# Paged sample attention: small loads issued in the sparse stage, keys turned in halves, branch rows combined in halves by VectorE and GpSimd

## What is computed

```python
sc = jnp.where((jnp.arange(n_keys)[None, :] <= qpos[:, None])[None], indexer_scores(qi, wi, ki_all), -jnp.inf)
_, sel = lax.top_k(sc, topk)                      # 256 of the 1028 keys of a request
kv_past = pool_kv[phys, sel_p % PAGE_SIZE]        # rows of the paged cache, phys from the page table
kv_sel = jnp.where(in_past[..., None, None, None], kv_past, kv_cur)
return sparse_attend(qa, kv_sel[:, :, :, 0], kv_sel[:, :, :, 1], valid)
```

```python
wts = jax.nn.softmax(jnp.stack(lses, axis=0), axis=0)
o = jnp.einsum('gbth,gbthd->bthd', wts, jnp.stack(outs, axis=0).astype(jnp.float32))
```

## Time and profile before

| | |
|---|---|
| median of 3 runs | 2304.71 us (2299.87 to 2311.17) |
| the profiled execution | 2307.14 us, of which the span is 2305.4 us |
| TensorE busy | 2114.3 us, 92% of the span |
| VectorE, ScalarE, GpSimd busy | 1175.4, 621.3, 518.2 us |
| mean granted TensorE clock | 0.943 of full speed |
| `attend_sample_a` | from about 1092.7 to 1185.1 us |

### The profile page before, as it was taken

How to read it: one execution, slowest core, us unless ns; L and a number is a source line. 1 busy time by engine, 2 the same in 40 slices (tenths; PEclk the granted TensorE clock), 3 DMA queues, 4 the chain that set the end, 5 groups by cost and what they waited for, 6 DMA issues and landing times. The chain is left out here.

```text
span 2305.4 us, 32999 instructions
## 1 busy us (share of the span) xinstructions
PE 2114.3 (92%) x12535; PEld 1945.7 (84%) x12535; DVE 1175.4 (51%) x2287; ACT 621.3 (27%) x1247; POOL 518.2 (22%) x569
## 2 busy tenths in 40 slices
PE   5999899999998976898669989989999999999997
PEld 5878788999998864555359988889999999999997
DVE  5049999998720413542337232644344444444445
ACT  5243222121210752343122233631121111111112
POOL 4786656778820001100000120210000000000000
PEclk9999999999986966999789998999999999999999
DMA  4122222357632444871337202030112110111001
GB/s 154 28 85 75 66 85 82 110 165 250 210 122 88 124 136 126 253 261 59 96 100 203 65 29 73 19 110 22 53 56 56 37 55 20 55 56 55 19 10 76
DMA packets 201025, 215.90 MB, mean 94 GB/s; under 512 B 47958, under 2 KB 186230, under 8 KB 200358
## 3 DMA queue, kind: packets, MB, share of 16 engines
q1 hardware_dynamic: 173206, 156.56, 23.1%
q10 hardware_dynamic: 26624, 29.87, 3.7%
q0 software_dynamic: 1040, 27.33, 3.5%
HBM read 178.94 MB, written 62.10 MB: 105 GB/s over the span
## 5 line engine op out<-in xcount | busy, mean ns | idle before, releaser
L3088 PE MATMUL p_g<-n_t_hi,g_hi 128*128 128x352 f32 x1056 | 342.4, 324 | 11.8 <-DVE g_lo L2980 8.9
L3088 PE MATMUL p_g<-n_t_lo,g_hi 128*128 128x352 f32 x1056 | 341.9, 324 | 0.0
L3088 PE MATMUL p_g<-n_t_hi,g_lo 128*128 128x352 f32 x1056 | 341.7, 324 | 0.0
L935 PE MATMUL pz<-w_hi,n_hi 128*128 128x384 f32 (+2 forms) x720 | 245.8, 341 | 0.4 <-issue 0.4
L935 PE MATMUL pz<-w_hi,n_lo 128*128 128x384 f32 (+2 forms) x720 | 239.6, 333 | 0.0
L935 PE MATMUL pz<-w_lo,n_hi 128*128 128x384 f32 (+2 forms) x720 | 239.4, 333 | 0.0
L3088 PEld LDWEIGHTS p_g<-n_t_hi,g_hi 128*128 128x128 f32 x1056 | 199.4, 189 | 13.0 <-issue 11.5
L843 DVE MATCH_REPLACE8 sel<-m,sel 128x1024 f32<-128x1024 f32 (+4 forms) x224 | 205.3, 921 | 0.0
L3088 PEld LDWEIGHTS p_g<-n_t_lo,g_hi 128*128 128x128 f32 x1056 | 199.4, 189 | 0.0
L3088 PEld LDWEIGHTS p_g<-n_t_hi,g_lo 128*128 128x128 f32 x1056 | 199.4, 189 | 0.0
L840 DVE MAX8 m<-sel 128x8 f32<-128x1024 f32 (+4 forms) x224 | 197.5, 925 | 0.2
(11 more groups left out here) (408 smaller groups left out, 4286.8 us busy)
## 6 DMA issues: line engine op xcount, KB each, us to landing
w_raw<-in_w_in SPq DMA_DIRECT2D x26, 768.0 KB, 4.6
relu<-z_qb SPq DMA_DIRECT2D x24, 512.0 KB, 5.2
w_first<-in_w_ffn_in SPq DMA_DIRECT2D x22, 512.0 KB, 6.7
g_raw<-in_w_ffn_in SPq DMA_DIRECT2D x22, 512.0 KB, 4.7
o_raw<-in_w_ffn_out SPq DMA_DIRECT2D x22, 512.0 KB, 4.1
z_b<-z ACTq DMA_DIRECT2D x48, 192.0 KB, 1.9
gates<-z ACTq DMA_DIRECT2D x48, 176.0 KB, 2.8
gate<-gates SPq DMA_DIRECT2D x24, 352.0 KB, 3.9
```

The source lines that it names most:

```text
L935: m = pe.matmul(out, tokens(a, k, i), b[:, n % 2, k, 0:w], start=(k == 0 and p == 0), stop=(k == KC - 1 and p == 2))
L3088: m = pe.matmul(p_g[:, t, e, 0:THIRD], a[:, u, e, w], b[:, k, t * THIRD:(t + 1) * THIRD], start=(k == 0 and p == 0), stop=(k == KC - 1 and ...
```

## The change

Seven small loads of `attend_sample_a` get buffers of their own, `early`, that live over both stages. Six of the loads are issued by SyncE at the end of the list of `attend_sparse`, which then waits for them; the page table is the one that `attend_sparse` loads anyhow, and the memset of `v_new` goes to that stage's GpSimd. The sample stage then begins without waits for loads on VectorE (query copies) and TensorE, and SyncE begins it with the branch loads, now six of half the tiles, followed by the late pages.

Keys are turned and copied by halves: `turn_half(b, c)` fills one bank of `p_x`, ScalarE copies 512 columns (`keys`), and `score_half` uses that half. TensorE turns a half of request `b + 1` ahead of each half of scores of request `b`.

The branch shares are made in two halves of four tiles (`shares`). ScalarE's two exponentials stand in its list behind the key copies of the requests 1 and 2. VectorE weights the first half, GpSimd the second. Two branch tiles (`BETWEEN` = 2) are turned between the scores and the values of each group of requests, the other four at the end, behind a wait for GpSimd.

```diff
@@ attend_sparse, sync
+                new = d["z_a"][SEQ:T, :]
+                sp.dma_start(early["ident"][:, :], d["ident"]).then_inc(s_early, 16)
...
+                sp.dma_start(early["q_row"][:, :, :], d["z_qa"].rearrange("r c -> (r c)").rearrange("(u p e) -> p u e", u=2, e=HD)).then_inc(s_early, 16)
+                sp.dma_start(early["k_new"][:, :], new[:, 512:640]).then_inc(s_early, 16)
+                sp.wait_ge(s_set, 1)
+                sp.dma_start(early["v_new"][0:NS, :], new[:, 640:768]).then_inc(s_early, 16)
                 sp.wait_ge(s_kv, 16 * PAGED * NPG)
+                sp.wait_ge(s_early, 16 * 6)
@@ attend_sample_a, scalar
-                act.wait_ge(s_diff, 1)
-                act.activation(ex[:, :, :, :], ex[:, :, :, :], ACT.Exp).then_inc(s_ex, 1)
...
+                def keys(b):
                     if b >= 2:
                         act.wait_ge(s_qk, b - 1)
+                    for c in range(2):
+                        act.wait_ge(s_kt, 2 * b + c + 1)
+                        act.activation(k_t[:, b % 2, 512 * c:512 * c + 512], p_x[:, c, :], ACT.Copy).then_inc(s_ktev, 1)
...
+                def shares(half):
+                    x = slice(HALF * half, HALF * (half + 1))
+                    act.wait_ge(s_diff, half + 1)
+                    act.activation(ex[:, :, x, :], ex[:, :, x, :], ACT.Exp).then_inc(s_ex, 1)
+
+                for u in range(2):
+                    for b in (range(5) if u == 0 else range(5, DB)):
+                        keys(b)
+                        if b in (1, 2):
+                            shares(b - 1)
+                    for i in range(BETWEEN * u, BETWEEN * (u + 1)):
+                        rest_high(i)
+                    weights(u)
@@ attend_sample_a, gpsimd
+                x = slice(HALF, NT)
+                pool.wait_ge(s_share, 2)
+                weighted(pool, 0, ob_row, 1)
+                weighted(pool, 1, term, 1).then_inc(s_gp, 1)
+                pool.wait_ge(s_gp, 1)
+                pool.tensor_tensor(ob_row[:, x, :], ob_row[:, x, :], term[:, x, :], ALU.add).then_inc(s_gp, 1)
+                pool.wait_ge(s_gp, 2)
+                weighted(pool, 2, term, 1).then_inc(s_gp, 1)
+                pool.wait_ge(s_gp, 3)
+                pool.tensor_tensor(ob_row[:, x, :], ob_row[:, x, :], term[:, x, :], ALU.add).then_inc(s_obrow[1], 1)
@@ attend_sample_a, vector
+                shares(0)
+                dve.wait_ge(s_share, 1)
+                weighted(dve, 0, ob_row, 0)
...
+                dve.tensor_tensor(ob_row[:, 0:HALF, :], ob_row[:, 0:HALF, :], term[:, 0:HALF, :], ALU.add).then_inc(s_obrow[0], 1)
+                shares(1)
...
+                for u in range(2):
+                    soft(u)
+                    for i in range(BETWEEN * u, BETWEEN * (u + 1)):
+                        rest_low(i)
+                    out(u)
+                for i in range(2 * BETWEEN, NT):
+                    rest_low(i)
@@ attend_sample_a, tensor
+                def turn_half(b, c):
...
                     if b:
-                        pe.wait_ge(s_ktev, b)
+                        pe.wait_ge(s_ktev, 2 * b + c - 1)
...
+                    for j in range(4):
+                        t = pe.transpose(p_x[:, c, j * P:(j + 1) * P], kv_of(b)[:, 4 * c + j, 0:P], ident[:, :])
...
+                for u in range(2):
+                    bias_and_new(u)
+                    for b in range(4 * u, 4 * u + 4):
                         for c in range(2):
+                            if b + 1 < DB:
+                                turn_half(b + 1, c)
+                            score_half(b, c)
+                    for i in range(BETWEEN * u, BETWEEN * (u + 1)):
+                        turn_rows(i)
+                    values(u)
+                for i in range(2 * BETWEEN, NT):
+                    turn_rows(i)
```

More of the change, by code:

```diff
@@ L1407, in attend_sparse @@
         rden = sb("rden_a", [P, 2, 4])
-        pages = sb("pages2", [1, DB * NPG], I32)
+        pages = early["pages"]
         p_s = ps("pa_s", [P, 2, 512])
@@ L1545, in _ @@
                 pool.memset(v_ext[:, :, :, HD:HD + 1], 1.0)
+                pool.memset(early["v_new"][:, :], 0.0)
                 pool.memset(nm_row[:, :, 0:HD], 0.0).then_inc(s_set, 1)
@@ L1730, in attend_sample_a @@
         sb, ps, sem = alloc(nc, ctx)
-        ident = sb("ident3", [P, P])
-        hmask = sb("hmask3", [P, AKV + BH])
-        row_exp = sb("row_exp3", [NS, 2, P])
+        ident, hmask, row_exp, q_row, k_new, v_new, pages = (early[x] for x in ("ident", "hmask", "row_exp", "q_row", "k_new", "v_new", "pages"))
         cb = sb("cb", [P, 3, NT, OBW])
@@ L1758, in attend_sample_a @@
         p_t = ps("p_t3", [P, 2, 512])
-        s_const = sem("b_const")
-        s_cb = sem("b_cb")
-        s_pages = sem("b_pages")
+        s_cb = [sem(f"b_cb{u}") for u in range(2)]
         s_kv = [sem(f"b_kv{b}") for b in range(DB - PAGED)]
-        s_q = sem("b_q")
         s_dv = sem("b_dv")
@@ L1767, in attend_sample_a @@
         s_ex = sem("b_ex")
-        s_obrow = sem("b_obrow")
+        s_obrow = [sem(f"b_obrow{u}") for u in range(2)]
+        s_share = sem("b_share")
+        s_gp = sem("b_gp")
         s_ct = sem("b_ct")
@@ L1790, in attend_sample_a, with weighted @@
         s_obs = sem("b_obs")
+        BETWEEN = 2
+        HALF = NT // 2
+        def weighted(eng, g, dst, half):
+            n = cb[:, g, :, 0:256].rearrange("p i (h e) -> p i h e", h=BH)
+            return [eng.tensor_tensor(dst[:, i, :].rearrange("p (h e) -> p h e", h=BH), n[:, i, :, :],
+                                      ex[:, g, i, :].unsqueeze(2).broadcast_to([P, BH, HD]), ALU.mult) for i in range(HALF * half, HALF * (half + 1))][-1]
         with nc.Block() as block:
@@ L1794, in _ @@
             def _(sp):
[L1795 to L1801, removed]
-                new = d["z_a"][SEQ:T, :]
-                sp.dma_start(k_new[:, :], new[:, 512:640]).then_inc(s_q, 16)
-                sp.wait_ge(s_pad, 1)
-                sp.dma_start(v_new[0:NS, :], new[:, 640:768]).then_inc(s_q, 16)
-                sp.wait_ge(s_pages, 16)
+                for half in range(2):
+                    x = slice(HALF * half, HALF * (half + 1))
+                    for g in range(3):
+                        sp.dma_start(cb[:, g, x, :], d["o_b"][g].rearrange("(i p) c -> p i c", p=P)[:, x, :]).then_inc(s_cb[half], 16)
                 for q in range(PAGED * NPG, DB * NPG):
@@ new lines, in turn_rows @@
+                def turn_rows(i):
+                    if i % HALF == 0:
+                        pe.wait_ge(s_obrow[i // HALF], 1)
+                    if i >= 2:
+                        pe.wait_ge(s_chi, i - 1)
+                        pe.wait_ge(s_clo, i - 1)
+                    if i >= BETWEEN:
+                        pe.wait_ge(s_ptev, 3 if i < 2 * BETWEEN else 6)
+                    for c in range(2):
+                        t = pe.transpose(p_t[:, i % 2, c * P:(c + 1) * P], ob_row[:, i, c * P:(c + 1) * P], ident[:, :])
+                    t.then_inc(s_ct, 1)
@@ L1999, in _ @@
[L1999 to L2007 removed]
+                turn_half(0, 0)
+                turn_half(0, 1)
```

162 lines of the change are left out of this document (66 added, 96 removed).

## The result

The changed kernel takes **2287.09 us**, the median of 8 runs (2282.72 to 2292.84), the kernel before on the same chip 2306.18 (8 runs, 2299.87 to 2316.89). The ratio is 0.9921, 95% interval 0.9902 to 0.9939: 14 to 23 us saved. The profiled execution has a span of 2282.3 us against 2305.4.

What follows compares the result with a forecast made beforehand. TensorE was taken to carry the stage, waiting for loads, key copies and branch-row turns. Terms 14.2 - 2.0 - 2.5 + 3.75 + 0.8 = 14.2, plus 1.0 for the clock, gave 15.2 us saved: 2289.5 us, range 2282 to 2299.

Steps and rivals of the forecast that it cites:

- Term 1: Opening of the sample stage: small loads issued early let query copies and TensorE start sooner, 14.2 us saved.
- Terms 2 and 3: First group: TensorE's stall on the second exponential gives back 2.0 us, the slow clock after it 2.5 us.
- term 3: Fourth request: TensorE restarts at slow clock after the stall, taking 5.45 us instead of 2.9; 2.5 us given back.
- Term 4: Second group's keys: three steps by halves take 2.8 us each instead of 4.05, 3.75 us saved.
- Values "unchanged": First group's values on TensorE were taken to last 11.6 us, as before.
- The 1.0 us for a shorter slow clock at the opening: TensorE's slow clock at the opening might last 7 us instead of 11.4; 1.0 of a possible 2.2 us counted saved.
- Term 5: End of the stage: four branch rows turned instead of eight, beside the chain of attention rows, 0.8 us saved.
- GpSimd hidden: GpSimd's weighting of the second half takes 15 us, ending near 1132, wanted only at about 1164.
- Rival (a): The clock helps more or the stall isn't there: 19 to 21 us saved, 2284 to 2286 us; chance 0.20.
- (b): The wait on the branch shares costs more: some 7 us go, 2297 us; chance 0.20.
- (c): The stage still ends on something fixed, so only half of term 1 arrives: 2300 us or so; chance 0.05.
- (d): TensorE's clock stays down through bursts cut into halves, 30 us more: 2320 us; chance 0.03.

Runs made afterwards that it cites:

- experiment 1: The kernel before with only the six small loads moved early into the sparse stage: stage 88.27 us, 2298.97 us, ratio 0.9983.
- experiment 3: The changed kernel with the second exponential of the shares behind the key copies of the fifth request: stage 69.93 us, 2282.68 us, ratio 0.9919.
- Experiment 4: The changed kernel with keys turned, copied and scored whole, as before: stage 77.13 us, 2286.54 us, ratio 0.9936.
- experiment 9: The changed kernel with VectorE's differences of both halves first, second shares behind the softmax, and 22 idle turns ahead of each values: stage 65.48 us, 2279.53 us.
- experiments 2 to 8 and 11: The changed kernel with one edit each to load place, engine order, key halves, branch rows or GpSimd work, or run once more: stages 69.93 to 78.82 us.
- experiment 6: The changed kernel with all eight branch rows turned at the end (BETWEEN = 0): stage 75.09 us in one run of 2288.85 us.
- experiment 10: The kernel of experiment 9 with 24 more idle turns at the sparse stage's end and 6 at the opening: stage 66.39 us, 2282.22 us, ratio 0.9891.
- experiments 9 and 12: The latter: experiment 10 with second-half differences behind the first half's weighting, second exponential behind the fifth request's key copies: stage 65.08 us, 2275.89 us.
- experiment 2: The changed kernel with the six small loads in the sample stage's own queue, ahead of the branch loads: stage 78.82 us, 2291.99 us, ratio 0.9936.

## Why the prediction was right

Forecast 2289.5 us, measured 2287.1; 15.2 us saved, measured 19.1 by the medians, 17.3 in the profiled stage. The mechanism was right in its main parts: the start of the queries, the new wait on the shares and its place, the gain of the second group and the hidden GpSimd. That the total came so close is in part luck: 1.0 us was counted for a clock that did not come back sooner, and 1.8 us came from values that were taken as unchanged. Term by term:

- **Term 1, the start of the queries: 14.2 forecast, 14.17 measured** (first turn of keys 16.55 to 2.38), and the loads in the stage ahead cost nothing that can be seen (from GpSimd's first memset of the sparse stage to the opening it is 203.0 us before and 203.5 now). What the prediction has wrong is "moving the loads removes it whole": the term needs two parts of the change, and experiment 1 shows 2.15 for the loads alone.
- **Terms 2 and 3, the wait on the second exponential and the clock in it: 4.5 forecast, 3.4 measured** (the gain falls from 14.17 at the keys to 10.77 at the softmax), and 3.67 by experiment 3. The mechanism and its place were as written: ScalarE's exponentials at +13.22 and +22.42 (forecast +13.1, +22.5), a wait of 5.80 ahead of the second ("some 6"), slow turns behind it. The size of the stall was off, 3.12 us instead of 4.7: TensorE was through the third request 1.3 us later than forecast, 0.7 of it because two steps took 3.13 us each and not 2.8, and went on 0.3 us sooner. The fourth request came back to full clock in its second half and took 4.75 us instead of 5.45, so term 3 alone is 1.6 us (over a step of 3.13) and not 2.5.
- **Term 4, the second group: 3.75 forecast, 3.83 measured**, right by two errors that cancel. **The price of 2.8 us a request was too low.** It counted half a turn as 0.5 and half a score as 0.92, as if the two ran on into each other; the rows show 1.57 for a half, 3.13 a request, some 0.15 more than the bare parts for each half. Three steps are then 1 us dearer than forecast. The group gained most of that back in its last three halves of scores, 1.91 us in a row where three at 0.92 were priced; that they overlap since two requests write different rows of `p_s` is argued, not shown. Experiment 4 bears out the sum of it, 4.0 us, and that the first group gains nothing by halves.
- **Values "unchanged" at 11.6 failed**: they took 10.26 and 10.80 us (before 11.60 and 11.26), 1.8 us of unforeseen gain. Their length is 8.87 us at full clock (experiment 9) and the rest goes with the length of a slow stretch (mean clock 0.83 and 0.75), which moves from run to run: 10.2 to 11.4 for the same list in experiments 2 to 8 and 11.
- **The 1.0 us for a shorter slow clock at the opening failed**: the clock was low until +13 (13.2 us at 0.51), not for 7 us from TensorE's start.
- **Term 5, the end: 0.8 forecast, 0.9 measured** (5.00 to 4.10), with TensorE waiting 1.94 us for `o_row` as the bound; in experiment 6, with all eight rows at the end, that wait is gone and the end takes 5.27 us.
- **GpSimd hidden: right**, though it took 11.9 us and not 15; the estimate from 740 ns a product was too dear (2.32 us for four).

The sum of what was measured, 14.17 - 3.40 + 1.34 + 3.83 + 0.46 + 0.90, is the 17.3 of the stage. Rival (a) held that the clock would help more; its time is within reach of the measurement, but not its reason, as the stall and its slow clock were there. Rivals (b), (c) and (d) fell: the loads of the first half landed at +8.9 with 4 us to spare, the gain arrived, and the second group's keys ran at 1.00.

## What to carry to other kernels

A wait for a load is worth only the distance to the next wait on the way: before moving a load, look at what stands in order on every engine between it and the work that counts; here an exponential on ScalarE held 12 of 14 us. Put an operation that waits for a slow chain behind all the copies that feed TensorE, not between them. And where TensorE idles for a few us inside a stage, look at what it pays afterwards: filling the waits with idle turns gained 3.2 to 4.7 us, about as much as turning and copying keys by halves (3.4 us of the stage). It is no guarantee, as the second group of experiment 10 shows.

## What the runs showed of the hardware

- **Idle work keeps the clock, mostly.** With waits of 2.5 to 6.4 us ahead of the values the clock fell to 1.2 GHz in every one of the 22 stretches without idle turns: in 14 during the wait, in 8 only 0.8 to 2.5 us into the values. With 22 turns of 2.57 us and 1.01 us of rest it stayed at 2.4 GHz in the four stretches of experiments 9 and 12, and in the second group of experiment 10 it fell all the same, 2.0 us into the values (in its first group, behind a wait of 3.93 us, it fell during the turns). The Trainium skill (TensorE: Matmul & The Clock Gate, HAM oscillation) tells of the fall after gaps, and the traces agree, but for the 8 stretches that began at full clock. That idle turns can prevent it, in four of the five gaps in which they ran at full clock, these runs add.
- **The clock does not follow the program alone.** Versions 10 and 12 have the same TensorE list up to the first group's softmax; in one the opening ran at full clock, in the other it fell 2.5 us in and stayed low to +12.7, and TensorE had the first group's scores 4.8 us later. Up to the fall the lists of all engines are the same; the two ran on different chips. Nor did it fall 0.7 us ahead of the opening in every run, as the expectation of experiment 10 says: in experiment 2 it fell 1.4 us behind it. The same skill page (Part 1) says that the number of slow products at a start differs from run to run; so a stage length may hold some us of clock that no edit explains.
- **The issue of a small load costs by its place**: 0.35 to 0.47 us each at the head of the queue in experiment 2, where the last of six landed by +4.0. Behind the branch loads of the kernel before, the issue of `q_row` alone took 3.34 us, and its landing 9.4 us:

```profile
1096.75 3.34 SPq L1801 DMA_DIRECT2D q_row<-z_qa  x1
```

- **VectorE beside GpSimd.** The 128x2 product of softmax took 0.23 us wherever GpSimd was idle, and 0.36 to 1.57 in the twelve cases beside its weighting. The changed kernel's two, then the longest, in experiment 4, with the sum of GpSimd beside it:

```profile
1120.56 0.38 DVE L1929 TENSOR_SCALAR st<-hmask_early,st 128x2 f32<-128x2 f32 x1
...
1147.41 0.23 DVE L1929 TENSOR_SCALAR st<-hmask_early,st 128x2 f32<-128x2 f32 x1
```

```profile
1114.10 2.35 POOL L1875 TENSOR_TENSOR ob_row<-ob_row,term 128x1024 f32<-128x1024 f32 x1
1114.91 1.57 DVE L1928 TENSOR_SCALAR st<-hmask_early,st 128x2 f32<-128x2 f32 x1
```

The scaling (1.23), the part of new keys (0.18) and the minimum (1.25) were the same in both. The Trainium skill (SBUF — State Buffer, Who interferes with whom) says that a VectorE product by scalars may take the port pair that it shares with GpSimd and that one of the two then waits for the other's whole instruction. The traces agree: in all twelve cases the small product ended 0.02 to 0.03 us behind the end of a GpSimd instruction, in ten the one that was running when it began, in two the next; in the rows above at 1116.48 against 1116.45. So its length is set by what GpSimd has at hand: 0.36 to 0.67 us beside products of 256 columns (0.61 each), 1.57 and 0.53 beside sums of 1024 (2.35). The wait is off the path here.
